# A two-layer trunk with expert gathers: scale rows spread by TensorE, six expert slots, two weight buffers, seven kept chunks

## The chip, the core and the metric

The kernel runs on one core of a Trainium2 chip. The metric is the device time of one execution in microseconds (us). A change of 0.2% (3.6 us) is about what a measurement of this kernel can tell from none.

## What is computed

The reference is one inference step of two layers for 256 prompt tokens and 32 sample tokens (model width 1024, all float32). Each layer is a token mixer followed by an expert mixer. Cut to what matters:

```python
# layer 0: chunk_mlp_mixer                      # layer 1: short_conv_mixer
z = gelu(rms_norm(x, norm_mix) @ w_in)          b_gate, c_gate, h = split(rms_norm(x, norm_mix) @ w_in, 3)
u, v = split(z, 2)                              z = c_gate * h
v = layer_norm(v, ln_g, ln_b)                   zp = concatenate([buf, z])
mixed = einsum('gij,bcjgd->bcigd', ws, v) + bias  conv = sum(conv_w[k] * zp[:, k:k + s_len] for k in range(3))
x = x + (u * mixed) @ w_out                     x = x + (b_gate * conv) @ w_out

def peer_ffn(h, ...):        # h = rms_norm(x, norm_ffn); both layers; every token, 8 heads, 16 experts of each
    q = h @ w_query                     # 8 heads x 2 halves x 128
    s = q . sub_keys                    # 128 scores per half
    idx, g = top 16 of the sums of the two halves' top 16, softmax
    a = gelu(sum over d of expert_u[idx] * h)
    x = x + sum over heads and k of g * a * expert_v[idx]
y = rms_norm(x, norm_final)
```

Outputs are y, the normalised v rows of the sample tokens, and the last two rows of the convolution's input for both groups.

## The kernel before

**Tiles and passes.** Tokens stand on partitions in three tiles: 0 and 1 with 128 prompt tokens each, 2 with the 32 sample tokens. The dense work is done in four passes: layer 0 for tile 0, layer 0 for tiles 1 and 2, then layer 1 in the same way (`PASSES`). Each pass streams its layer's weight matrices as chunks of 1024 x 256 floats, 1 MiB each: 32 chunks in layer 0 (8 for v, 8 for u, 8 for the way out, 8 for the queries), 24 in layer 1 (12 for b, c and h, 4, 8).

**Where weights lie.** `kept` holds the first chunk of a layer for both passes of the layer (`KEEP = 1`). All others go through `wring`, three buffers of 1 MiB; SyncE issues each load as soon as TensorE has used the chunk three places earlier (`load_chunk`, line 527). Before the experts start, chunks 1 to 5 of the first pass lie in slots of `uvring`.

**Experts.** Each of 576 items (tile, head, rank) is a gather by GpSimd of 128 rows of 8 KB (an expert's u and v side by side), 1 MiB in all, into one of seven slots of `uvring` (`RING = 7`, line 585). For an item VectorE takes the dot product of u and the token (`dot`, line 1139), ScalarE its gelu (line 879), VectorE makes a small diagonal matrix of the weight (line 1152), and TensorE adds weight times v into PSUM (`weigh`, line 632; line 624 for tile 2). Then the slot is free, and GpSimd gathers the item seven places on.

**Order of the work.** The program runs in turns of two items (`TURNS`). `plan_steps` deals the dense work and the routing (top 16, softmax, indices) out over the turns before it is built: in each turn every engine first does its part of the two items and then dense steps up to a budget (`ROOM`). Each engine runs its list in order. In a turn TensorE's list is: two items' matmuls, then dense matmuls, typically one weight chunk. PSUM has six banks for the dense groups, used in rotation, and two for the experts' sum.

**Scale rows.** The gains of the root-mean-square norms come as broadcast DMAs of 512 KB (one row to 128 partitions) into `gain`, five in all (lines 554, 563, 564, 570, 894). Gain and bias of the layer norm of v come the same way: 1 MiB each for tile 0 into two slots of `uvring`, and for tiles 1 and 2 in halves into `ln_half`, whose second half ScalarE's queue loads only once VectorE has used the first (`ln_load`, the step `ln load`); VectorE waits for it in `lnapply` (lines 1060 and 1063). A norm is a sum of squares (`nstat`), a root on ScalarE, and `napply` (line 1035). The bias of the mixing matrix is a matmul of `ones` with `brow`.

**Names of the dense steps.** `v`, `vq`, `vf` are the products for v (`vq` the sample tokens' in quarters of the array, `vf` the sum of the quarters); `u`, `bch`, `q` go through `blocks` (line 643), two blocks to a chunk; `mix` is the mixing over positions, `out`, `oq`, `of` the way out (line 747), `xT` a transpose, `s` the scores.

Of the kernel before, what the change touches and what calls it, by code (L numbers as in the profile page):

```python
# [39 lines left out]
WRING = 3  # L40
# [11 lines left out]


KEEP = 1
EARLY = KEEP + 5
RINGED = [n for n in range(EARLY, PASS_CHUNK0[-1]) if n - max(p for p in PASS_CHUNK0 if p <= n) >= KEEP]

RING = 7  # L60
# [5 lines left out]
PAIRS = len(ITEMS) // 2  # L66
END = {(l, t): (ITEM0[l, t] + TILE_ITEMS[t]) // 2 - 1 for l, t in ITEM0}
# [29 lines left out]
def mixer_steps(n):  # L97
# [22 lines left out]
    if l == 0:  # L120
# [11 lines left out]
        for b in range(KA):  # L132
            out.append(("PE", ("u", n, b), blk, [x_read]))
            out.append(("ACT", ("u read", n, b), 0.35, [("u", n, b)]))
            if b == 0:
# [6 lines left out]
                for h in range(2):  # L142
                    for t in tiles:
                        out.append(("DVE", ("lnapply", t, h), 2.8, [("root", "ln", 0, t), ("ln load", n, h)]))
                    if n == 1 and h == 0:
                        out.append(("ACT", ("ln load", n, 1), 0.1, [("lnapply", tiles[-1], 0)]))
# [32 lines left out]
    if 2 in tiles:  # L179
        out.append(("ACT", ("spread", l), 3.2, [("napply", "ffn", l, 2)]))  # L180
# [22 lines left out]
def final_steps(t):  # L203
    return [("DVE", ("nstat", "final", 1, t), 1.5, [("vdone", 1, t)]),
            ("ACT", ("root", "final", 1, t), 1.6, [("nstat", "final", 1, t)]),
            ("DVE", ("napply", "final", 1, t), 1.6, [("root", "final", 1, t)])]
# [5 lines left out]
        "mix": "gate", "out": "add", "vq": "vq read", "vf": "vf read", "oq": "oq read", "of": "add"}  # L212
# [23 lines left out]
def plan_steps():  # L236
# [3 lines left out]
    norms = [s for s in early if not s[1][0].startswith("xT")]  # L240
# [13 lines left out]
    turn = {("start",): -2, ("ln load", 0, 0): -2, ("ln load", 0, 1): -2, ("ln load", 1, 0): -2}  # L254
# [1018 lines left out]
```

## Time and profile before

| what | value |
|---|---|
| median of 3 runs | 1820.49 us (1819.88 to 1820.83) |
| the profiled execution | 1821.85 us, span 1820.0 us |
| moved by DMA | 733.21 MB, mean 403 GB/s |
| TensorE busy | 1334.9 us (73%) |
| VectorE busy | 1218.0 us (67%) |
| ScalarE, GpSimd busy | 290.2 us, 683.7 us |
| mean granted TensorE clock | 0.79 of full speed |

Busy times of different engines overlap. The profile's page gives each engine's busy share in 40 slices of the span, the bytes that each DMA queue moved, and the chain of work that ended last. A busy TensorE is not one at its peak. "Idle before" an instruction is the time that its engine stood still, with what ended it.

### The profile page before, as it was taken

To read this page: it belongs to the slowest core of one execution; us is meant where nothing else is said; L and a number is where in the kernel's file an instruction comes from. 1 tells how busy PE (TensorE), PEld (TensorE's weight loads), DVE (VectorE), ACT (ScalarE), POOL (GpSimd) and SP (SyncE) were. 2 spreads that over 40 slices of the span, in tenths; PEclk is the share of its full clock that TensorE was granted. 3 is DMA by queue.
4 is the path that set the end of the run, shared out by engine and by line. 5 is a ranking of instruction groups with operands and counts; after the bars stand their busy time and mean duration, and the time that the engine had idled before them with its cause. 6 is when DMAs were issued, how large, how long until landed. Compare 5 with 4: busy or idle time off the path is not lost.

```text
span 1820.0 us, 22838 instructions
## 1 busy us (share of the span) xinstructions
PE 1334.9 (73%) x8328; PEld 636.3 (35%) x8328; DVE 1218.0 (67%) x3189; ACT 290.2 (16%) x972; POOL 683.7 (38%) x580
## 2 busy tenths in 40 slices
PE   7996988978847888766664598878766667776743
PEld 6984546535502554421111175346211111111100
DVE  1338676756679577688887646656888975555565
ACT  1112221103202102111121111031111110000011
POOL 0013332343334333334445533443544444444453
PEclk9998999998967988976665599989766666666655
DMA  9779999999999999999999999999999999999996
GB/s 352 276 276 422 421 421 393 398 421 421 420 421 385 419 421 421 421 419 401 421 421 390 399 416 421 422 420 421 402 421 409 412 422 421 421 421 417 418 412 278
DMA packets 103267, 733.21 MB, mean 403 GB/s; under 512 B 12305, under 2 KB 12817, under 8 KB 14930
## 3 DMA queue, kind: packets, MB, share of 16 engines
q0 software_dynamic: 82944, 604.02, 80.4%
q1 hardware_dynamic: 19442, 125.82, 17.2%
q10 hardware_dynamic: 768, 1.91, 0.3%
q8 instruction: 66, 1.08, 0.2%
q14 instruction: 47, 0.39, 0.1%
HBM read 730.19 MB, written 1.52 MB: 402 GB/s over the span
## 4 chain that ended last, share of the span: by engine, by line
DMA 56%; PE 26%; DVE 8%; issue 7%; DVEq 2%; POOL 2%; ACT 0%; ACTq 0%; POOLq 0%
DMA uvring<-expert_uv_dram,idx 54%; PE psum L632 11%; PE psum L643 7%; PE psum L747 3%; PE psum L675 2%; POOL uvring L585 2%; DVE diag L1152 1%; DVE uvring L1139 1%; DMA arena<-ln_bias_dram 1%; DVEq L953 1%; PE psum L624 1%; PE psum L727 1%; DVE ti L955 1%; PE psum L730 1%; PE psum L665 0%
## 5 line engine op out<-in xcount | busy, mean ns | idle before, releaser
L585 POOL DMA_INDIRECT uvring<-expert_uv_dram,idx x576 | 683.5, 1187 | 1114.5 <-PE psum L632 878.2
L1139 DVE SCALAR_TENSOR_TENSOR uvring<-uvring,xn 128x1024 f32<-128x1024 f32 x576 | 705.7, 1225 | 458.9 <-DMA uvring<-expert_uv_dram,idx 448.5
L632 PE MATMUL psum<-uvring,diag 64*64 64x512 f32 x4096 | 725.7, 805 | 367.8 <-DVE diag L1152 358.4
L632 PEld LDWEIGHTS psum<-uvring,diag 64*64 64x64 f32 x4096 | 134.6, 159 | 872.5 <-DVE diag L1152 811.3
L879 ACT ACTIVATE a_gelu<-a_raw 128x1 f32<-128x1 f32 x576 | 116.6, 203 | 1335.4 <-DVE uvring L1139 1334.9
L643 PEld LDWEIGHTS psum<-xT,wring 128*128 128x128 f32 x2240 | 296.1, 200 | 50.8 <-issue 47.4
L643 PE MATMUL psum<-xT,wring 128*128 128x128 f32 (+1 forms) x2240 | 309.9, 299 | 3.2 <-ACT arena L798 2.0
L1152 DVE TENSOR_SCALAR diag<-twin,a_gelu,gate 128x64 f32<-128x64 f32 x512 | 159.1, 311 | 0.4 <-ACT a_gelu L879 0.4
L624 PE MATMUL psum<-uvring,diag 128*32 128x256 f32 x512 | 67.8, 624 | 91.7 <-DVE diag L1152 85.6
L747 PE MATMUL psum<-wring,arena 128*128 128x256 f32 x384 | 88.4, 387 | 0.6 <-issue 0.6
L747 PEld LDWEIGHTS psum<-wring,arena 128*128 128x128 f32 x384 | 72.2, 192 | 21.9 <-issue 12.5
L798 ACT ACTIVATE arena<-psum 128x128 f32<-128x128 f32 (+2 forms) x164 | 45.9, 301 | 119.7 <-PE psum L643 78.9
L624 PEld LDWEIGHTS psum<-uvring,diag 128*32 128x32 f32 x512 | 13.0, 139 | 145.9 <-DVE diag L1152 137.9
L1139 DVE DVE_READ_ACCUMULATOR uvring<-uvring,xn 128x1 f32 x576 | 47.4, 82 | 0.0
L879 ACT ACT_TABLE_LOAD x29 | 37.2, 1283 | 0.5
L675 PE MATMUL psum<-wring,xT 128*128 128x256 f32 x144 | 33.1, 385 | 0.0
L675 PEld LDWEIGHTS psum<-wring,xT 128*128 128x128 f32 x144 | 26.9, 190 | 7.8 <-issue 4.5
L1044 DVE BATCH_NORM_STATS2 stats<-arena 128x6 f32<-128x512 f32 (+1 forms) x12 | 7.4, 674 | 32.2 <-ACT arena L798 32.2
L1118 DVE TENSOR_TENSOR x<-x,psum 128x256 f32<-128x256 f32 (+1 forms) x24 | 9.9, 412 | 27.6 <-PE psum L747 27.6
L665 PE MATMUL psum<-ident,xn 128*128 128x128 f32 (+1 forms) x96 | 16.7, 329 | 12.0 <-DVE xn L1035 11.9
L873 ACT ACT_TABLE_LOAD x19 | 24.4, 1283 | 0.3
L1072 DVE TENSOR_TENSOR arena<-arena,psum 128x256 f32<-128x256 f32 (+1 forms) x16 | 7.0, 452 | 25.7 <-PE psum L730 25.7
(104 smaller groups left out, 718.8 us busy)
## 6 DMA issues: line engine op xcount, KB each, us to landing
wring<-w_chunks_dram SPq DMA_DIRECT2D x103, 1024.0 KB, 9.5
uvring<-expert_uv_dram,idx POOLq DMA_INDIRECT x576, 12.0
uvring<-w_chunks_dram SPq DMA_DIRECT2D x5, 1024.0 KB, 13.9
kept<-w_chunks_dram SPq DMA_DIRECT2D x2, 1024.0 KB, 10.8
gain<-gains_dram SPq DMA_DIRECT2D x4, 512.0 KB, 13.1
x<-x_tok_dram SPq DMA_DIRECT2D x2, 512.0 KB, 5.0
uvring<-ln_gain_dram SPq DMA_DIRECT2D x1, 1024.0 KB, 26.6
uvring<-ln_bias_dram SPq DMA_DIRECT2D x1, 1024.0 KB, 27.4
```

What stands on the lines that cost most here:

```text
L585: pool.indirect_dma_start(uvring[:, n % RING, :], None, expert_uv, bass.IndirectOffsetOnAxis(ap=idx[t][:, i:i + 1], axis=0),).then_inc(uv_ ...
L624: mm = nc.tensor.matmul(acc[32 * q:32 * q + 32, 0:256], diag[:, place % DIAGS, 0:32], row[:, D + 256 * q:D + 256 * (q + 1)], start=first, ...
L632: mm = nc.tensor.matmul(acc[64 * j:64 * j + 64, 512 * i:512 * (i + 1)], diag[64 * i:64 * i + 64, place % DIAGS, :], row[64 * i:64 * i + 64 ...
L643: mm = nc.tensor.matmul(bank(key, WIDTH[n]), w[:, k, j * P:(j + 1) * P], act[:, k, 0:cols], start=(k == 0), stop=(k == KD - 1))
L675: mm = nc.tensor.matmul(bank(k, WCOLS, ROWS[t]), xT[:, kk, LCOL[t]:LCOL[t] + ROWS[t]], w[:, kk, :], start=(kk == 0), stop=(kk == KD - 1))
L727: nc.tensor.matmul(both[:, :, cols], ones[0:r, :], bias, start=True, stop=False)
L747: mm = nc.tensor.matmul(bank(key, WCOLS, ROWS[t]), act[:, h * KD + kk, LCOL[t]:LCOL[t] + ROWS[t]], w[:, kk, :], start=(h == 0 and kk == 0) ...
L798: nc.scalar.activation(out, bank(key, n, rows), func).then_inc(scalar_read, 1)
L873: nc.scalar.activation(gate[t][:, c], gate[t][:, c], ACT.Exp, accum_out=esum[t][:, h:h + 1]).then_inc(exp_done, 1)
L879: nc.scalar.activation(a_gelu[:, c:c + 1], a_raw[:, c:c + 1], ACT.Gelu_apprx_tanh).then_inc(gelu_done, 1)
L1139: nc.vector.scalar_tensor_tensor(out=uvring[:, slot, 0:D], in0=uvring[:, slot, 0:D], scalar=1.0, in1=xn[t][:, :], op0=ALU.mult, op1=ALU.mu ...
L1152: nc.vector.tensor_scalar(diag[:, place % DIAGS, 0:32 if t == 2 else 64], fold[:, :] if t == 2 else twin[:, :], a_gelu[:, c:c + 1], gate[t ...
```

## The change

1. **Scale rows by TensorE.** One DMA of 256 KB on ScalarE's queue puts all the rows (five gains, the layer norm's gain and bias in halves, the mixing bias) into 64 unused partitions of `x[2]`, the `table`. A matmul with one column of the identity, broadcast, as the stationary side spreads 512 elements of a row over 128 partitions of a PSUM bank (steps `gb` for gains, `lnb` for the layer norm of tiles 1 and 2). `napply` and the new `lnrow` read the scale from PSUM; `lnrow` does tiles 1 and 2 together, 512 columns at a time. The gain broadcasts and the halves of the layer norm's rows are gone. Tile 0 keeps its layer norm broadcasts.
2. **Smaller arena.** `gain`, `ones`, `brow`, `tril`, `zeros`, `quarters` and `ln_half` are gone or lie in other buffers; v of tile 2 lies in kept chunk 0; the convolution's product is made in place and two columns are carried from tile 0 to tile 1.
3. **Weights.** `KEEP` goes from 1 to 7, `WRING` from 3 to 2, `RING` from 7 to 6. `plan_homes` puts chunks 7 to 23 of the first pass, and chunk 26, in the slots of `uvring` and in the two buffers in turn; GpSimd waits for the last chunk of a slot before its first gather there.
4. `quarters` shares `turned`, so ScalarE waits for the readers of the one before it writes the other.

```diff
-WRING = 3
+WRING = 2
-KEEP = 1
-EARLY = KEEP + 5
+KEEP = 7
-RING = 7
+RING = 6
+def plan_homes():
+    places = [("slot", s) for s in range(2, RING)] + [("ring", r) for r in range(WRING)]
+    home, uses, ringed = [], {}, 0
+    for n in range(PASS_CHUNK0[-1]):
+        c = n - max(p for p in PASS_CHUNK0 if p <= n)
+        if c < KEEP:
+            at = ("kept", c)
+        elif n < 24:
+            at = places[(n - KEEP) % len(places)]
+        elif n == 26:
+            at = ("slot", RING - 1)
+        else:
+            at, ringed = ("ring", ringed % WRING), ringed + 1
...
     def norm(which, behind):
...
-            out.append(("DVE", ("napply", which, l, t), 1.6, [("root", which, l, t)]))
+        for j in range(2):
+            out.append(("PE", ("gb", which, l, tiles[0], j), 0.9, []))
+            out.append(("DVE", ("napply", which, l, tiles[0], j), 0.7 * len(tiles),
+                        [("gb", which, l, tiles[0], j), ("root", which, l, tiles[-1])]))
...
+            if n == 1 and 3 <= b < 11:
+                q, a = divmod(b - 3, 2)
+                out.append(("PE", ("lnb", q, a), 0.9, []))
+                out.append(("DVE", ("lnrow", q, a), 1.4, [("lnb", q, a), ("root", "ln", 0, 2)]))
...
+            def row_of(r, cols):
+                pe.wait_ge(ident_landed, 16)
+                pe.wait_ge(rows_landed, 16)
+                return ident[64:P, 64 + r:65 + r].to_broadcast([64, P]), table[:, cols]
...
+                    open_group(k)
+                    matrix, values = row_of(r, slice(j * 512, (j + 1) * 512))
+                    nc.tensor.matmul(bank(k), matrix, values, start=True, stop=True).then_inc(group_done, 1)
...
+                    wait_group(dve, key)
+                    if a == 1:
+                        after(steps[0])
+                        dve.wait_ge(vector_read, G["lnb", q, 0][3])
+                    for t in (1, 2):
+                        r = ROWS[t]
+                        done = nc.vector.scalar_tensor_tensor(
+                            out=v[t][0:r, cols], in0=v[t][0:r, cols],
+                            scalar=rstd[0:r, t:t + 1] if a else mv[0:r, t, 0:1], in1=bank(key, rows=r),
+                            op0=ALU.mult if a else ALU.subtract, op1=ALU.add if a else ALU.mult)
...
-            act.dma_start(gain[:, 0, :], gains[0:1, :].partition_broadcast(P)).then_inc(gain_landed[0], 16)
+            act.dma_start(table, rows).then_inc(rows_landed, 16)
```

**SyncE's queue.** These are its loads from the first 42 in a row to the last gain row, before: the rest of the first two passes' chunks, two gain rows, layer 1's keys and chunks.

```order
L527 DMA wring<-w_chunks_dram 128x2048 x42
L563 DMA gain<-gains_dram 128x1024
L564 DMA gain<-gains_dram 128x1024
L566 DMA keys<-sub_keys_dram 128x2048
L522 DMA kept<-w_chunks_dram 128x2048
L527 DMA wring<-w_chunks_dram 128x2048 x46
L570 DMA gain<-gains_dram 128x1024
```

The same place now:

```order
L557 DMA uvring<-w_chunks_dram 128x2048
L557 DMA wring<-w_chunks_dram 128x2048 x30
L582 DMA keys<-sub_keys_dram 128x2048
L557 DMA kept<-w_chunks_dram 128x2048 x7
L557 DMA wring<-w_chunks_dram 128x2048 x34
L587 DMA y_tok_dram<-xn 128x1024 x2
```

Seven kept chunks are loaded together behind the keys, then 34 through the ring where there were 46. Over the whole program 98 chunks are loaded instead of 110.

**TensorE's list in pass two, the start of the products for v**, before (line 632 is two items' matmuls in one turn):

```order
L675 MATMUL psum<-kept,xT 128x256 x8
L651 MATMUL psum<-kept,xT 32x256 x8
L632 MATMUL psum<-uvring,diag 64x512 x8
L675 MATMUL psum<-wring,xT 128x256 x8
L651 MATMUL psum<-wring,xT 32x256 x8
L632 MATMUL psum<-uvring,diag 64x512 x8
```

and now (line 649 is the former 632):

```order
L692 MATMUL psum<-kept,xT 128x256 x8
L668 MATMUL psum<-kept,xT 32x256 x8
L649 MATMUL psum<-uvring,diag 64x512 x8
L692 MATMUL psum<-kept,xT 128x256 x8
L668 MATMUL psum<-kept,xT 32x256 x8
L649 MATMUL psum<-uvring,diag 64x512 x8
```

The order is the same, and the chunk comes from `kept` for the first seven.

**TensorE's list in pass two, the products for u, now**, where the `lnb` matmuls (line 731) stand:

```order
L660 MATMUL psum<-xT,wring 128x160 x8
L731 MATMUL psum<-x,ident 128x512
L660 MATMUL psum<-xT,wring 128x160 x8
L649 MATMUL psum<-uvring,diag 64x512 x8
L731 MATMUL psum<-x,ident 128x512
L660 MATMUL psum<-xT,wring 128x160 x8
L731 MATMUL psum<-x,ident 128x512
```

Eight such matmuls come between the blocks, where before there was none; a turn has one or two of them.

## Rows read from the trace of the kernel before

**Rows 1.** The page: DMA share in 40 slices, bytes
```profile
DMA  9779999999999999999999999999999999999996
...
DMA packets 103267, 733.21 MB, mean 403 GB/s; under 512 B 12305, under 2 KB 12817, under 8 KB 14930
```

**Rows 2.** The page: the chain that ended last, by engine
```profile
DMA 56%; PE 26%; DVE 8%; issue 7%; DVEq 2%; POOL 2%; ACT 0%; ACTq 0%; POOLq 0%
```

**Rows 3.** Stretches: length, busy by engine, TensorE's clock, DMA share, GB/s
```profile
0.00:128.50 128.50, 113.24 (x703) 103.56 (x704) 38.12 (x110) 20.13 (x48) 0.21 (x5) 0.99 0.80 296
128.50:1808.00 1679.50, 1218.89 (x7607) 532.19 (x7609) 1173.85 (x3067) 267.30 (x918) 683.45 (x576) 0.78 1.00 414
...
1500.00:1600.00 100.00, 71.80 (x320) 10.98 (x312) 58.18 (x118) 7.91 (x39) 42.40 (x39) 0.61 1.01 421
```

**Rows 4.** Stretches of dense work in passes two, two, three and four
```profile
172.90:250.60 77.70, 73.93 (x532) 42.32 (x528) 54.22 (x155) 16.73 (x53) 27.25 (x24) 1.00 1.01 420
250.60:335.10 84.50, 71.39 (x484) 49.80 (x480) 57.37 (x134) 15.22 (x48) 24.22 (x23) 0.91 0.99 406
567.30:663.80 96.50, 83.25 (x616) 57.09 (x616) 65.55 (x183) 17.32 (x62) 30.48 (x28) 0.87 0.99 405
1031.40:1128.60 97.20, 88.05 (x616) 60.72 (x616) 52.68 (x135) 15.83 (x60) 35.23 (x28) 0.92 0.99 409
```

**Rows 5.** Stretches between them, where layer 1's chunks are loaded ahead
```profile
492.00:552.00 60.00, 31.98 (x152) 5.62 (x152) 42.17 (x120) 7.79 (x27) 20.51 (x18) 0.60 1.01 418
776.00:800.00 24.00, 15.99 (x105) 7.14 (x104) 17.05 (x53) 2.50 (x11) 7.88 (x7) 0.78 1.01 421
```

**Rows 6.** TensorE's timeline: two blocks in pass four, two items in pass three
```profile
1052.51 4.62 PE L643 MATMUL psum<-xT,wring 128*128 128x160 f32 x32
590.86 1.95 PE L632 MATMUL psum<-uvring,diag 64*64 64x512 f32 x16
```

**Rows 7.** VectorE's timeline at the layer norm's second half
```profile
289.33 1.28 DVE L1060 SCALAR_TENSOR_TENSOR arena<-arena,mv 128x1024 f32<-128x1024 f32 x1 [11.46 <-DMA arena<-ln_bias_dram]
```

**Rows 8.** DMA issues between 1031.4 and 1128.6 us, median time to landing
```profile
wring<-w_chunks_dram SPq DMA_DIRECT2D x11, 1024.0 KB, 9.1
```

**Rows 9.** Time to landing, chunk at 106.9 us, then chunk at 189.2 us
```profile
DMA to landing us min/median/max: 4.7/4.7/4.7
...
DMA to landing us min/median/max: 9.2/9.2/9.2
```

**Rows 10.** Gathers at 1500 to 1600 us, then the gather at 335.1 us
```profile
DMA to landing us min/median/max: 10.8/11.1/12.0
DMA to landing us min/median/max: 6.5/6.5/6.5
```

**Rows 11.** Timeline at 1528 us: a dot product, and the gather it leads to
```profile
1528.39 1.23 DVE L1139 SCALAR_TENSOR_TENSOR uvring<-uvring,xn 128x1024 f32<-128x1024 f32 x1 [1.02 <-DMA uvring<-expert_uv_dram,idx]
...
1532.19 0.95 POOL L585 DMA_INDIRECT uvring<-expert_uv_dram,idx  x1 [1.77 <-PE psum L632]
```

**Rows 12.** TensorE's timeline: the first transposes, and those before the queries
```profile
9.32 1.97 PE L665 MATMUL psum<-ident,xn 128*128 128x128 f32 x8 [9.32 <-DVE xn L1035]
109.48 1.31 PE L665 MATMUL psum<-ident,xn 128*128 128x128 f32 x8 [2.58 <-DVE xn L1035]
```

**Rows 13.** TensorE's timeline: one product of 512 columns (two records)
```profile
194.57 1.05 PE L702 MATMUL psum<-quarters,fold 128*32 128x512 f32 x2
```

**Rows 14.** Stretches with the DMA engines below their rate, columns as in rows 3
```profile
330.00:350.00 20.00, 18.40 (x125) 9.69 (x123) 15.54 (x50) 1.60 (x7) 5.35 (x6) 0.91 0.96 367
570.00:580.00 10.00, 6.94 (x40) 2.25 (x36) 9.78 (x32) 2.39 (x7) 3.23 (x3) 0.56 0.82 316
960.00:970.00 10.00, 6.36 (x48) 2.39 (x48) 9.62 (x20) 3.80 (x10) 5.83 (x6) 0.67 0.85 301
1040.00:1050.00 10.00, 10.00 (x61) 5.87 (x54) 7.02 (x15) 1.44 (x7) 6.98 (x4) 0.68 0.81 306
1270.00:1280.00 10.00, 10.00 (x71) 6.99 (x70) 8.11 (x14) 2.26 (x9) 3.32 (x3) 0.92 0.89 356
```

More of the change, by code:

```diff
@@ L141, in mixer_steps @@
                     out.append(("ACT", ("root", "ln", 0, t), 1.6, [("lnstat", t)]))
[L142 to L146, printed above, removed]
+                for h in range(2 if n == 0 else 0):
+                    out.append(("DVE", ("lnapply", 0, h), 2.8, [("root", "ln", 0, 0)]))
+            if n == 1 and 3 <= b < 11:
+                q, a = divmod(b - 3, 2)
+                out.append(("PE", ("lnb", q, a), 0.9, []))
+                out.append(("DVE", ("lnrow", q, a), 1.4, [("lnb", q, a), ("root", "ln", 0, 2)]))
         if n == 0:
@@ L211 @@
 READ = {"xT": "xT read", "v": "v read", "u": "u read", "bch": "bch read", "q": "q read", "s": "s read",
-        "mix": "gate", "out": "add", "vq": "vq read", "vf": "vf read", "oq": "oq read", "of": "add"}
+        "mix": "gate", "out": "add", "vq": "vq read", "vf": "vf read", "oq": "oq read", "of": "add",
+        "gb": "napply", "lnb": "lnrow"}
 def group_of(k):
@@ L244, in plan_steps @@
     ahead = first[:cut] + route_steps(0, 0, 0)
-    at = [k for _, k, _, _ in ahead].index(("out", 0, 0, 0, 0))
-    ahead[at:at] = norms
-    dense = first[cut:] + [s for s in early if s not in norms]
+    at = [k for _, k, _, _ in ahead].index(("xT read", 0, "ffn", 0, 1)) + 1
+    ahead[at:at] = stats
+    dense = first[cut:] + [s for s in early if s not in stats]
     dense += [s for s in mixer_steps(1) if s not in early] + mixer_steps(2) + mixer_steps(3)
@@ L316 @@
 EXPS = [h for k in planned("ACT", ("exp",)) for h in ((k[1], k[2], k[3] + j) for j in range(dict(calls_of(*k[1:3]))[k[3]]))]
-FORM = {r: g for g, r in READ.items() if r not in ("gate", "add")}
+FORM = {r: g for g, r in READ.items() if r not in ("gate", "add", "napply", "lnrow")}
 PE_STEPS = tuple(READ)
@@ L326, in plan_groups @@
     vector = {}
-    for k in planned("DVE", ("gate", "add")):
-        vector[("of", *k[1:3]) if k[0] == "add" and k[3] == 2 else
-               ("mix" if k[0] == "gate" else "out", *k[1:])] = len(vector) + 1
+    form = {"gate": "mix", "add": "out", "napply": "gb", "lnrow": "lnb"}
+    for k in planned("DVE", tuple(form)):
+        vector[("of", *k[1:3]) if k[0] == "add" and k[3] == 2 else (form[k[0]], *k[1:])] = len(vector) + 1
     for k in planned("PE", PE_STEPS):
```

271 lines of the change are left out of this document (136 added, 135 removed).

## The prediction

> **What bounds the kernel now.** I read the page first, then stretches by engine, then timelines where two engines meet. The page shows the DMA engines nearly full in almost every slice after the fourth [rows 1], and the chain that ended last is 56% DMA, 26% TensorE [rows 2]. Split at the first gather, 128.5 us, the stretches say more [rows 3]. Before it DMA moves 296 GB/s and TensorE is busy 113 of 128.5 us: the first pass waits for TensorE. From there to 1808 us DMA moves 414 GB/s, and 421 where nothing else happens, so 421 is the rate here and 1 MiB takes 2.49 us. Only 1679.5 x (1 - 414/421) = 28 us of DMA time are unused there.
>
> That reads as a DMA-bound kernel, but the dense stretches have a second bound right behind it [rows 4]. TensorE is busy 73.9 of 77.7 us where v is computed in pass two, 71.4 of 84.5 in the u part, 83.3 of 96.5 and 88.1 of 97.2 where b, c and h are computed in passes three and four. A turn there is 4.62 us of blocks and 1.95 us for two items [rows 6], about 6.5 us, while its two gathers and one chunk need 3 x 2.49 = 7.5 us of DMA. With the chunk kept, DMA needs 5.0 us and TensorE still 6.5. So bytes taken from a dense turn give back at most 1 us of their 2.49, and bytes moved out of it into a stretch with gathers alone cost all 2.49.
>
> **The change part by part.** It takes out twelve chunks (12.58 MB) and nine broadcasts of 0.524 MB, and adds 0.26 MB: 17.0 MB, 40.5 us of DMA. What that is worth, place by place, in us, with both ends:
>
> *Start and first pass: +1.2 (0 to +3).* Two spreading matmuls stand ahead of the first transposes. A product of 512 columns takes 1.05 us [rows 13], and the first transposes run 1.97/1.31 = 1.5 times slower than later ones [rows 12], so 1.6 us each, partly beside the wait for x and VectorE's sum. The gain broadcast no longer competes with x. Later the first query chunk can only be loaded when the last chunk of the way out is used, at 106.9 us; it lands 4.7 us later [rows 9], 111.6, about when the queries start (transposes at 109.48 plus some 2 us). The gain matmuls there run while TensorE waits for the norm. DMA bytes before 128.5 us are not on the path.
>
> *One chunk less ahead of the v part: -1.5 (-2.5 to 0).* Two buffers are filled there, not three; VectorE is also busy.
>
> *v part: -3 (-3.8 to 0).* The kept chunks leave TensorE's list as it was, and it has 3.8 us of idle time [rows 4].
>
> *u part and layer norm: -4 (-4.7 to 0).* VectorE's wait of 11.46 us for the bias half [rows 7] goes with its DMA. Eight spreading matmuls add 8 x 1.05 = 8.4 us to TensorE: 79.8 of 84.5. `lnrow` costs VectorE about 1 us more in shorter instructions, hidden (57.4 busy of 84.5). What is late next is TensorE.
>
> *Three gain rows after the first gather: -3.7.* 3 x 0.524 MB at 421 GB/s, in full stretches. The other two gain rows and the first two layer norm halves lie before 128.5 us: nothing.
>
> *Layer 1's chunks loaded ahead: +12.4 (+10 to +12.4).* Behind the keys SyncE now issues seven kept and two ring chunks, where it issued one and three. DMA moves 418 GB/s there [rows 5], so five more cost 5 x 2.49. They come out of the next stretch.
>
> *b, c, h in pass three: -9.5 (-13.2 to -5).* Of about eleven loads there five remain, beside the 28 gathers (POOL, [rows 4]): 28 + 5 transfers are 82 us, TensorE's 83.3 is the floor under 96.5. I take 87, since both engines are near full and take turns at waiting.
>
> *One ring chunk less before pass four: -2.5*, at 421 GB/s [rows 5].
>
> *b, c, h in pass four: -4.5 (-9.1 to 0).* Eleven loads [rows 8] become five, TensorE's floor is 88.1 of 97.2; more of it is one engine's work in a row than in pass three.
>
> *Six slots: +8 (0 to +12.4).* In the gather-only stretch a landed item leads to the next gather 3.8 us later (1528.39 to 1532.19, [rows 11]), which lands 11.1 us after its issue [rows 10]: 14.9 us for six items, because an item's slot is freed only after the next item's dot product. With six slots it is 12.4 us for five items, so the landing may take 8.6 us. A gather behind an empty queue took 6.5 [rows 10], so the steady state holds, with 2.1 us to spare where it had 4.6. Where VectorE is late by more, the DMA engines stand still: they lost 12 us in five places before [rows 14], by their GB/s against 421. Each can grow by one slot, 5 x 2.49 = 12.4. I take two thirds, as one of the five is the layer norm's wake.
>
> *Two weight buffers: +2 (0 to +8).* A chunk beside gathers lands after 9.2 us even when it is the only one asked for, against 4.7 without gathers [rows 9]. Two turns must cover its landing and its own use: (9.2 + 4.6)/2 = 6.9 us, a little over TensorE's 6.5 and under DMA's 7.5. About ten turns run at TensorE's pace: 10 x 0.4 = 4, half of it absorbed. The Trainium skill (DMA: Bandwidth & Descriptors, Queues, rings and completion order) says that each DMA engine serves the queues that have work in rotation, packet by packet. By that rule a lone chunk beside gathers would take about twice its transfer time, two buffers would cost nothing and the sum would be 2 us lower; no row here shows such a short landing beside gathers, so the row's value stands.
>
> Sum: 1.2 - 1.5 - 3 - 4 - 3.7 + 12.4 - 9.5 - 2.5 - 4.5 + 8 + 2 = **-5.1 us**. The profiled execution took 1821.85 us (span 1820.0) and would take 1816.8; against the median of the runs, 1820.49, it is **1815.4 us**.
>
> **The rivals.**
>
> *All bytes count.* DMA is the only bound, and TensorE's busy time shrinks with fewer stalls. For it: 421 GB/s everywhere, and TensorE's records stretch where its clock is low (0.87 in pass three, [rows 4]). Against it: 73.9 of 77.7 us at a clock of 1.00. After the first gather eleven chunks and five broadcasts go, 14.2 MB, 33.6 us; with 1.2 at the start it gives 1788 us.
>
> *Slower: the sixth slot was needed.* The place is the loop of [rows 11], in every item. It decides from the landing of a gather with five slots in flight: above 8.6 us each item costs a fifth of the excess. Lowest seen is 6.5 after an empty queue, but a chunk beside gathers needs 9.2. At 8.8 us it is 0.04 x 576 = 23 us; with the other terms less the 8 already in, -13.1 + 23 gives 1830 us. Late routing on VectorE works the same way. For it: VectorE's 9.6 to 9.8 of 10 us busy where DMA runs dry [rows 14]. Against it: the spare 2.1 us.
>
> *The rows from TensorE are waited for.* `lnrow` and `napply` stand in VectorE's list and now wait for a matmul that stands behind a turn of dense work on TensorE; dot products queue behind them. If that eats the u part's gain, the same time is lost at six norms, 1 us each: 4 + 6 = +10 less what is hidden, about 1820 us, no change. It is also the case in which the change does not do what it says: the broadcasts' wait is only replaced.
>
> **How the numbers follow.** The forecast gets 0.46 (own range 1806 to 1822; 0.36 of it faster, 0.10 within), all bytes 0.16, the sixth slot 0.28, the replaced wait 0.10 (0.04 within, 0.06 slower). Of the sixth slot's cases 0.01 end within. The bound for faster and slower is 0.2%, 3.6 us, about what a measurement of this kernel can tell from no change: faster 0.52, same 0.15, slower 0.33. The range 1796 to 1835 takes in the ends of the unknown terms; it leaves out most of the bytes case (0.12) and the top of the slower one (0.08).
>
> **What would show it.** Right: DMA moves about 716 MB; the v part keeps its length within 4 us with DMA well under 421 GB/s and TensorE full; 1031 to 1129 shortens by under 6 us; the wait for the bias half is gone; the stretch after the keys is 10 us and more longer; gathers land after some 8.6 us in the gather-only stretch, at 2.49 us an item. Wrong: the dense stretches shorten by 10 us and more each (bytes), or the gather-only stretch shows more than 2.5 us an item and GpSimd's gathers find idle DMA engines (sixth slot), or VectorE shows waits for line 731 of several us.

## The result, and the profile after

The changed kernel takes 1842.43 us (median of 4 runs, 1839.28 to 1848.51); the kernel before, on the same chip, 1820.18 us (4 runs, 1819.8 to 1820.83). The ratio is 1.012, with a 95% interval of 1.0103 to 1.0137: slower by 22 us, where 5 us less were forecast and the range ended at 1835.

The page after, whose first lines answer to [rows 1] and whose last one to [rows 2] (DMA share and GB/s in 40 slices, bytes, queues, chain by engine):

```profile
DMA  9749999899999999999999999999999999999997
GB/s 377 280 175 418 357 357 385 353 409 415 394 421 406 372 418 420 420 409 396 402 396 403 416 335 398 413 413 406 399 417 400 378 419 421 421 421 416 417 415 303
DMA packets 100369, 716.17 MB, mean 390 GB/s; under 512 B 12032, under 2 KB 12544, under 8 KB 13568
q0 software_dynamic: 82944, 604.02, 81.1%
q1 hardware_dynamic: 16896, 110.09, 14.8%
DMA 44%; PE 36%; DVE 9%; issue 8%; DVEq 2%; POOL 1%; ACT 0%; SPq 0%; POOLq 0%
```

The bytes came out as forecast, 716 MB. The rate did not hold: 390 GB/s in the mean where it was 403. At 421 GB/s the 17.0 MB saved would be 40 us, but the time in which the DMA engines stand idle grew by more than that. The span less the bytes at 421 GB/s is 1820.0 - 1741.6 = 78 us before and 1837.5 - 1701.1 = 136 us now.

Stretches, columns as in [rows 3]: up to the first gather, from there to the last, and 100 us of gathers alone.

```profile
0.00:130.00 130.00, 120.19 (x712) 103.84 (x713) 34.05 (x102) 20.12 (x48) 0.25 (x5) 1.00 0.71 276
130.00:1826.00 1696.00, 1235.94 (x7663) 541.17 (x7661) 1179.90 (x3083) 266.70 (x916) 681.06 (x576) 0.78 0.99 401
1520.00:1620.00 100.00, 69.32 (x324) 11.00 (x320) 59.00 (x121) 8.11 (x40) 44.09 (x40) 0.65 1.01 421
```

With gathers alone nothing is lost: 40 gathers in 100 us and 421 GB/s, as before. The loss is in the rest, 401 GB/s from 130 to 1826 us against 414.

For the place of it, take turns (two items each) and read when VectorE starts the dot product of a turn's first item. Lengths of the stretches between such turns in the profiled executions, in us; K is the number of kept chunks, W of weight buffers, R of slots. The rows below the second are the experiments.

| kernel (K, W, R) | to 0 | 0-16 | 16-32 | 32-56 | 56-64 | 64-80 | 80-144 | 144-160 | 160-216 | 216-287 | span |
|---|---|---|---|---|---|---|---|---|---|---|---|
| before (1, 3, 7) | 134.3 | 111.6 | 116.6 | 160.5 | 40.6 | 111.8 | 353.2 | 109.7 | 309.4 | 358.6 | 1820.0 |
| after (7, 2, 6) | 135.8 | 101.4 | 123.2 | 169.0 | 53.4 | 100.8 | 358.9 | 105.1 | 318.2 | 357.8 | 1837.5 |
| e1 (6, 3, 6) | 136.8 | 101.7 | 116.7 | 165.4 | 53.3 | 103.8 | 358.8 | 107.4 | 318.3 | 359.2 | 1835.0 |
| e2 (6, 2, 7) | 136.3 | 98.6 | 132.3 | 160.8 | 53.3 | 101.1 | 351.7 | 101.3 | 313.9 | 356.8 | 1820.1 |
| e3 (5, 3, 7) | 136.4 | 97.9 | 116.4 | 159.4 | 52.7 | 102.5 | 352.8 | 105.9 | 309.6 | 357.4 | 1805.0 |
| e4 (1, 3, 7) | 136.3 | 106.6 | 114.4 | 157.7 | 42.9 | 110.6 | 354.4 | 111.3 | 306.7 | 356.8 | 1811.7 |
| e5 (6, 2, 6) | 135.6 | 101.9 | 126.4 | 168.0 | 50.7 | 105.2 | 359.6 | 105.8 | 324.7 | 358.3 | 1850.2 |
| e7 (4, 3, 8) | 135.7 | 100.6 | 125.0 | 154.7 | 50.9 | 103.0 | 354.1 | 104.1 | 309.2 | 357.5 | 1808.9 |
| e8 (5, 3, 7) spread | 135.8 | 97.6 | 127.5 | 159.1 | 41.6 | 104.6 | 352.4 | 105.9 | 311.2 | 357.2 | 1807.0 |
| e10 (5, 2, 7) | 135.8 | 98.1 | 127.8 | 161.6 | 50.2 | 101.3 | 353.8 | 102.9 | 314.4 | 356.5 | 1816.5 |
| e11 (4, 4, 7) | 134.5 | 103.5 | 123.3 | 156.4 | 53.3 | 105.3 | 352.2 | 106.2 | 306.3 | 357.1 | 1812.0 |
| e12 (1, 2, 6) | 136.9 | 112.7 | 121.9 | 164.5 | 40.7 | 112.8 | 361.9 | 111.0 | 317.8 | 358.3 | 1852.2 |
| e6 before, six slots | 133.2 | 117.7 | 116.9 | 164.4 | 41.9 | 116.6 | 353.6 | 111.4 | 317.5 | 358.4 | 1845.4 |
| e9 before, two buffers | 153.3 | 112.1 | 121.7 | 159.7 | 40.0 | 113.2 | 351.8 | 110.5 | 312.4 | 357.6 | 1845.9 |

Turns 0 to 32 hold pass two's dense work, 64 to 80 pass three's, 144 to 160 pass four's; layer 1's chunks are loaded in 56 to 64; 216 to 287 are gathers alone. After against before: 0 to 16, 64 to 80 and 144 to 160 get shorter (-10.2, -11.0, -4.6), 56 to 64 grows by 12.8, and 16 to 32, 32 to 56, 80 to 144 and 160 to 216 grow by 6.6, 8.5, 5.7 and 8.8. The forecast had a gain for the first, and for all the places of [rows 14] together no more than the 8 us of the slots.

Two waits. VectorE from 240 to 300 us, where [rows 7] had 11.46 us for the bias half, and TensorE's chunk matmuls in all, then in 135 to 375 us:

```profile
DVE uvring L1190 <- DMA uvring<-expert_uv_dram,idx: 15.4, 10, 3.4
DVE arena L1109 <- PE psum L731: 2.5, 3, 1.2
DVE diag L1203 <- ACT a_gelu L908: 0.3, 1, 0.3
```
```profile
PE psum L660 <- DMA wring<-w_chunks_dram: 21.0, 14, 4.1
...
PE psum L660 <- DMA wring<-w_chunks_dram: 10.7, 4, 4.1
```

The wait for the bias is gone, and what takes its place is 2.5 us for the spreading matmul. But TensorE now waits 21.0 us for chunks, half of it in the u part. So there were three suspects: two buffers, six slots, or the rows from TensorE with their new order.

### The profile page after: what moved, and what is told of

Read it like the earlier page. It is cut to its first block, busy times and chain, and to the rows that moved or that the text cites. A ratio compares the mean times of both kernels' runs of the same rounds, so it can differ in the third digit from the quotient of the medians.

```text
span 1837.5 us, 22998 instructions
## 1 busy us (share of the span) xinstructions
PE 1358.2 (74%) x8388; PEld 645.6 (35%) x8388; DVE 1220.0 (66%) x3197; ACT 289.6 (16%) x970; POOL 681.3 (37%) x580
## 4 chain that ended last, share of the span: by engine, by line
DMA 44%; PE 36%; DVE 9%; issue 8%; DVEq 2%; POOL 1%; ACT 0%; SPq 0%; POOLq 0%
DMA uvring<-expert_uv_dram,idx 39%; PE psum L660 12%; PE psum L649 12%; DMA wring<-w_chunks_dram 4%; PE psum L779 4%; PE psum L692 3%; DVE uvring L1190 2%; DVE diag L1203 2%; PE psum L731 1%; PE psum L641 1%; PE psum L762 1%; PE psum L759 1%; PE psum L668 1%; POOL uvring L601 1%; DVE ti L998 1%
## 5 line engine op out<-in xcount | busy, mean ns | idle before, releaser
L649 PE MATMUL psum<-uvring,diag 64*64 64x512 f32 x4096 | 709.0, 795 | 337.5 <-DVE diag L1203 325.5
L908 ACT ACTIVATE a_gelu<-a_raw 128x1 f32<-128x1 f32 x576 | 116.6, 203 | 1320.2 <-DVE uvring L1190 1307.6
L660 PE MATMUL psum<-xT,wring 128*128 128x160 f32 (+1 forms) x1632 | 228.8, 299 | 22.4 <-DMA wring<-w_chunks_dram 21.0
L660 PEld LDWEIGHTS psum<-xT,wring 128*128 128x128 f32 x1632 | 215.4, 197 | 63.6 <-issue 29.9
L779 PE MATMUL psum<-wring,arena 128*128 128x256 f32 x304 | 76.0, 407 | 1.8 <-issue 1.0
L828 ACT ACTIVATE arena<-psum 128x160 f32<-128x160 f32 (+2 forms) x160 | 45.8, 295 | 148.0 <-PE psum L660 107.5
L660 PEld LDWEIGHTS psum<-xT,kept 128*128 128x128 f32 x448 | 56.1, 191 | 11.8 <-issue 9.7
L660 PE MATMUL psum<-xT,kept 128*128 128x128 f32 (+1 forms) x448 | 59.2, 291 | 0.4 <-ACT xT L846 0.4
L692 PE MATMUL psum<-kept,xT 128*128 128x256 f32 x224 | 52.5, 394 | 0.8 <-ACT xT L846 0.8
L692 PEld LDWEIGHTS psum<-kept,xT 128*128 128x128 f32 x224 | 43.4, 197 | 11.9 <-issue 6.0
L731 PE MATMUL psum<-x,ident 64*128 64x512 f32 x60 | 34.1, 684 | 6.0 <-DMA ident<-ident_c_dram 6.0
```

What stands on the lines that cost most here:

```text
L649: mm = nc.tensor.matmul(acc[64 * j:64 * j + 64, 512 * i:512 * (i + 1)], diag[64 * i:64 * i + 64, place % DIAGS, :], row[64 * i:64 * i + 64 ...
L660: mm = nc.tensor.matmul(bank(key, WIDTH[n]), w[:, k, j * P:(j + 1) * P], act[:, k, 0:cols], start=(k == 0), stop=(k == KD - 1))
L692: mm = nc.tensor.matmul(bank(k, WCOLS, ROWS[t]), xT[:, kk, LCOL[t]:LCOL[t] + ROWS[t]], w[:, kk, :], start=(kk == 0), stop=(kk == KD - 1))
L731: nc.tensor.matmul(bank(k), matrix, values, start=True, stop=True).then_inc(group_done, 1)
L779: mm = nc.tensor.matmul(bank(key, WCOLS, ROWS[t]), act[:, h * KD + kk, LCOL[t]:LCOL[t] + ROWS[t]], w[:, kk, :], start=(h == 0 and kk == 0) ...
L828: nc.scalar.activation(out, bank(key, n, rows), func).then_inc(scalar_read, 1)
```

## The experiments

Times are medians; a difference "to before" is taken with the kernel before in the same series on the same chip (1821.58, 1822.47, 1823.4 and 1820.89 us for e1-e4, e5-e8, e9-e11, e12). The changed kernel has room for 15 units of 8 KB a partition as kept chunks, buffers and slots, so e1 to e3 trade one against another. The intervals are wide beside the smaller effects: some 7 us either way for e1, 2 to 6 for the others, so a difference of two runs under some 5 us is not clear of the noise.

### e1: the third buffer back

```diff
-WRING = 2
+WRING = 3
-KEEP = 7
+KEEP = 6
```

> The changed kernel with three weight buffers again, paid for with one kept chunk less (six kept, six slots for expert rows). Theory 1, the two weight buffers cost most of the loss: the changed kernel's TensorE waits 21 us in sum for chunks of the weight ring, and its turns 16 to 56 lost 15 us where 8 us of gain were forecast; most of it comes back, and the time falls by 12 to 22 us to 1820 to 1830 us, with the wait for chunks at lines 660 and 731 under 8 us. Theory 2, the six slots cost most of it: the time falls by less than 6 us (over 1836 us). Theory 3, the rows spread by TensorE and the new order of the steps cost it: also less than 6 us. The kept chunk that is given up is worth under 2 us by all of them.

1838.09 us (1834.61 to 1849.5), ratio 1.0107 (1.0067 to 1.0147), 16.5 to before. Only 5.7 of the 22 us come back, less than theory 1 had said. The waits are gone (the matmul's idle time of 22.4 us becomes 2.5), so the buffers may matter, but they are not the main cause:

```profile
L660 PE MATMUL psum<-xT,wring 128*128 128x160 f32 (+1 forms) x1728 | 239.2, 297 | 2.5 <-ACT arena L828 1.4
```

### e2: the seventh slot back

```diff
-KEEP = 7
+KEEP = 6
-RING = 6
+RING = 7
```

> The changed kernel with seven slots for expert rows again, paid for with one kept chunk less (six kept, two weight buffers). Theory 2, the six slots cost most: turns 80 to 144 and 160 to 216, where gathers run with little beside them, lost 15 us; they come back, and the time falls by 12 to 18 us to 1824 to 1830 us. Theory 1, the two weight buffers: the time falls by less than 6 us, and the waits of TensorE for chunks of the weight ring stay at about 20 us. Theory 3: less than 6 us.

1817.66 us (1813.2 to 1824.76), ratio 0.9984 (0.9963 to 1.0006). One slot for one kept chunk is worth 26 us, more than theory 2 had said.

### e3: both back

```diff
-WRING = 2
+WRING = 3
-KEEP = 7
+KEEP = 5
-RING = 6
+RING = 7
```

> The changed kernel with three weight buffers and seven slots, paid for with two kept chunks (five kept). By theories 1 and 2 together the losses of both come back: 1842 less 15 to 20 for the buffers and 8 to 15 for the slots is 1807 to 1819 us, faster than the kernel before. By theory 3, the rows spread by TensorE or the order of the steps as the cause, it stays over 1830 us.

1806.17 us (1803.08 to 1811.68), ratio 0.9918 (0.9893 to 0.9944): faster than the kernel before by 15 us, a little under the expected range, and with e7 the best of the study. Theory 3 alone would have left it over 1830. Its page, in the same lines:

```profile
GB/s 382 296 162 422 383 412 420 404 416 421 409 423 401 393 421 421 420 421 415 420 409 400 420 351 421 412 421 419 406 419 410 390 420 422 422 421 420 422 416 281
DMA packets 100945, 720.37 MB, mean 399 GB/s; under 512 B 12096, under 2 KB 12608, under 8 KB 13632
```

It moves 4.2 MB more than the changed kernel, 10 us of DMA, and is 38 us faster (15.4 under the kernel before, where the changed one is 22.3 over it).

### e4: the change without the trade

```diff
-WRING = 2
+WRING = 3
-KEEP = 7
+KEEP = 1
-RING = 6
+RING = 7
```

> The changed kernel with the memory as it was: one kept chunk, three weight buffers, seven slots, so that only the rows spread by TensorE, the smaller arena and the new order of the steps are left of the change. Theories 1 and 2: the loss was in the memory that was traded, so this is at or a little under the kernel before, 1810 to 1822 us. Theory 3: over 1828 us. Against the run with five kept chunks it tells what four more kept chunks are worth: the prediction's terms say 12.4 x 4/6 of loss at the keys against (9.5 + 4.5) x 4/6 of gain in passes three and four, so within 2 us of each other.

1813.25 us (1812.81 to 1815.89), ratio 0.9957 (0.9941 to 0.9974). Theory 3 falls: the rows from TensorE, the smaller arena and the new order together save 8.3 us. Which of them does it was not tested. Its second part missed: four more kept chunks (e3 against e4) are worth 7.1 us, not within 2.

### e5: six kept, two buffers, six slots

```diff
-KEEP = 7
+KEEP = 6
```

> The changed kernel with one kept chunk less and nothing for it: six kept, two weight buffers, six slots, so that it differs from the run with the seventh slot by the slot alone and from the run with the third buffer by the buffer alone. Theory 2, refined: the seventh slot is worth 22 to 28 us and the third buffer 2 to 6, the seventh kept chunk under 3, so 1840 to 1846 us. Rival: the seven kept chunks themselves were the loss in the changed kernel, and giving one up is what both runs gained by: then 1825 to 1836 us.

1848.96 us (1844.21 to 1853.45), ratio 1.0137 (1.0106 to 1.0167), 26.5 to before. That is over the 1840 to 1846 us expected. Against e2 this is one slot alone: 30.4 us (22 to 28 expected). Against e1 it is one buffer alone: 10.0 us (2 to 6 expected), a difference that is hardly clear of e1's wide interval. The seventh kept chunk comes out at 4.2, which is not clear of the noise. The rival, seven kept chunks as the loss, is out.

The slot's mechanism can be read here. About the same piece of the program, turns 104 to 112 (routing, items, no chunk loads), first with six slots, then with seven (columns as in [rows 3]); the second line of each is 5 us inside it:

```profile
838.00:880.00 42.00, 26.24 (x126) 4.88 (x128) 35.49 (x109) 3.99 (x17) 18.80 (x16) 0.62 0.96 387
864.00:869.00 5.00, 4.24 (x24) 0.75 (x16) 4.85 (x13) 0.41 (x2) 3.12 (x3) 0.65 0.59 206
```
```profile
832.00:872.00 40.00, 23.34 (x128) 4.51 (x128) 35.68 (x109) 3.82 (x17) 20.04 (x15) 0.71 1.01 418
856.00:861.00 5.00, 4.18 (x28) 0.86 (x24) 4.81 (x14) 0.59 (x3) 3.24 (x3) 0.84 1.03 411
```

DMA falls to 206 GB/s in the one and stays at 411 in the other. The timelines of VectorE, TensorE and GpSimd with six slots say why (start, length, in brackets the idle time before and its releaser):

```profile
856.59 0.09 DVE L992 MATCH_VALUE_LOAD scores<-tv,scores 128x8 f32 x1
...
859.60 0.29 DVE L998 FIND_INDEX8 ti<-tv,scores 128x8 uint32<-128x128 f32 x1
859.96 1.23 DVE L1190 SCALAR_TENSOR_TENSOR uvring<-uvring,xn 128x1024 f32<-128x1024 f32 x1
```
```profile
856.73 1.98 PE L649 MATMUL psum<-uvring,diag 64*64 64x512 f32 x8 [0.26 <-DVE diag L1203]
861.48 6.77 PE L649 MATMUL psum<-uvring,diag 64*64 64x512 f32 x32 [2.77 <-DVE diag L1203]
869.68 1.09 PE L649 MATMUL psum<-uvring,diag 64*64 64x512 f32 x8 [1.44 <-DVE diag L1203]
```
```profile
859.02 0.94 POOL L601 DMA_INDIRECT uvring<-expert_uv_dram,idx  x1 [1.31 <-PE psum L649]
865.26 1.77 POOL L601 DMA_INDIRECT uvring<-expert_uv_dram,idx  x1 [5.31 <-PE psum L649]
867.34 0.94 POOL L601 DMA_INDIRECT uvring<-expert_uv_dram,idx  x1 [0.30 <-PE psum L649]
```

From 856.59 to 859.89 VectorE finds top values for the next head, and the dot product behind it starts only at 859.96, 3.4 us after the first of them. TensorE then takes 1.98 us an item at a low clock, where it takes 1.09 at full clock. No slot comes free, and GpSimd issues nothing for 6.2 us (859.02 to 865.26). With six slots that empties the queue. With seven one more gather lies in it, and the longest pause of GpSimd's at this place is 4.3 us. A part of this one place is TensorE's clock and not the slot: over the 42 and 40 us it is 0.62 in the one and 0.71 in the other. Counted in slices of 1 us, over turns 32 to 144 and 160 to 216, spells in which at least 0.5 us of transfer at 421 GB/s is missing: e5 has 31 with 34.8 us, e2 has 11 with 9.8 us. These turns are 21 groups of 16 items, so with six slots most groups have a spell. The 25 us between the two kernels are most of the 30. How many spells there are depends on the shortfall from which a slice counts; that six slots have at least twice as many does not.

The kernel before and e6, which differ by the slot alone, show that the engines are late about as often, and that the ring decides what it costs. In the same turns GpSimd's issues lie more than 4 us apart 76 times before and 80 times in e6, and at most 7.2 and 7.3 us apart, at a mean granted clock of 0.79 and 0.78; spells, with slices from a tenth short, are 9 with 11 us before and 22 with 23 us in e6.

The steady state is as the prediction had it. Gathers from 1560 to 1660 us, issue to landing, with six slots and then, for e2, with seven; both at 421 GB/s:

```profile
uvring<-expert_uv_dram,idx POOLq DMA_INDIRECT x41, 8.6
```
```profile
uvring<-expert_uv_dram,idx POOLq DMA_INDIRECT x40, 11.4
```

### e6: the kernel before with six slots

```diff
-EARLY = KEEP + 5
+EARLY = KEEP + 4
-RING = 7
+RING = 6
```

> The kernel before with six slots instead of seven and nothing else (one chunk of the first pass goes to the weight ring instead of a slot). Theory: a slot less costs wherever TensorE or VectorE is late by more than the ring covers, in the kernel before as in the changed one: 22 to 32 us more, 1842 to 1852 us, with most of it in the dense stretches and little between turns 232 and 280. Rival: the sixth slot was only missed because two weight buffers made TensorE late: under 10 us more, 1821 to 1831 us.

1847.86 us (1842.83 to 1852.87), ratio 1.0138 (1.0107 to 1.0169), 25.4 to before. The slot's price is no matter of this change's other parts. In the profiled executions 12.6 us of it lie in turns 0 to 16, 64 to 80 and 144 to 160, where TensorE is dense, and 12.0 in 32 to 56 and 160 to 216; "most in the dense stretches" was half right. Turns 216 to 287 give none of it (358.4 against 358.6).

### e7: eight slots

```diff
-WRING = 2
+WRING = 3
-KEEP = 7
+KEEP = 4
-RING = 6
+RING = 8
```

> The changed kernel with four kept chunks, three weight buffers and eight slots. If a slot buys cover for the time that the engines are late, an eighth buys less than the seventh but still some: 5 to 12 us off the run with seven slots and five kept (1806.2), less 2 for the kept chunk, so 1796 to 1803 us. Rival: with seven the queue is full nearly everywhere (its slices show 400 to 421 GB/s), and an eighth is worth nothing: 1806 to 1810 us.

1806.41 us (1802.08 to 1810.69), ratio 0.9901 (0.9879 to 0.9924): the same as e3, with one kept chunk less. The rival's number, but not cleanly: the profiled execution lost 8.6 us against e3 in turns 16 to 32, where TensorE's clock fell (last section), and after turn 32 it is 6.8 us shorter than e3. Whether an eighth slot is worth a few us stays open.

### e8: layer 1's kept chunks loaded earlier

e3, with kept chunks 1 to 4 of layer 1 loaded between pass two's chunks:

```diff
             for n in range(PREFETCHED, PASS_CHUNK0[2]):
                 load_chunk(n)
+                if PASS_CHUNK0[1] + 10 <= n < PASS_CHUNK0[1] + 9 + KEEP:
+                    load_chunk(PASS_CHUNK0[2] + n - PASS_CHUNK0[1] - 9)
...
-            for n in range(PASS_CHUNK0[2], PASS_CHUNK0[4]):
+            for n in (PASS_CHUNK0[2], *range(PASS_CHUNK0[2] + KEEP, PASS_CHUNK0[4])):
```

> The changed kernel with five kept chunks, three buffers and seven slots, and the kept chunks of layer 1 but the first loaded one by one between the chunks of pass two's u and out parts instead of in a row behind the keys. The loads in a row delayed the gathers by 12 us between turns 56 and 64. Theory A: the queue has slack in pass two, where it moves 391 to 416 GB/s, and part of the 10 us of these four chunks comes for nothing: 1796 to 1803 us. Theory B: bytes cost the same wherever they go, since gathers are behind all the time: 1804 to 1808 us, with the loss moved to turns 24 to 48.

1807.7 us (1803.79 to 1814.04), ratio 0.9919 (0.9887 to 0.9951): theory B. Turns 56 to 64 shorten by 11.1 us (52.7 to 41.6) and turns 16 to 32 grow by 11.1 (116.4 to 127.5), somewhat earlier than the turns 24 to 48 expected. There was no slack; the gathers give way to the loads wherever those stand: from 266 to 296 us, at 421 and 419 GB/s, GpSimd issues 7 gathers where it issued 10 in e3.

### e9: the kernel before with two buffers

```diff
-WRING = 3
+WRING = 2
```

> The kernel before with two weight buffers instead of three and nothing else. Theory B: where TensorE runs one chunk after another (the u, q and b, c, h parts) it takes about 9.2 us a chunk (two blocks of 4.62) and a chunk lands 9 to 10 us after its issue beside gathers; with two buffers every late landing becomes a wait of TensorE, and its granted clock falls in it. Waits of the chunk matmuls for the weight ring go from near 0 to over 20 us, and the time rises by 8 to 20 us, to 1830 to 1842 us. Rival, the rule of the prediction (two buffers cost 2): 1820 to 1826 us.

1847.45 us (1842.5 to 1849.26), ratio 1.0124 (1.0102 to 1.0146), 24.1 to before: more than either theory allowed (8 to 20 us by theory B). 19.0 us of it lie ahead of turn 0, where this kernel's first pass loads all but six chunks through the ring; the changed kernel's slots avoid just that. The rest is mainly 5.1 us in turns 16 to 32 and 3.0 in 160 to 216. TensorE's wait is there, 48.9 us in sum:

```profile
PE psum L643 <- DMA wring<-w_chunks_dram: 48.9, 31, 5.8
```

### e10: two buffers with five kept chunks

```diff
-KEEP = 7
+KEEP = 5
-RING = 6
+RING = 7
```

> The changed kernel with five kept chunks and seven slots, as in the run with both back, but with two weight buffers: against that run (1806.2) the buffer alone. Theory B: 8 to 20 us more, 1814 to 1826 us, most of it lost in turns 16 to 32 (shorter by 15 or more us with three buffers in the pair compared so far) with the wait of line 660 for the weight ring at over 20 us. Rival: the third buffer gave nothing by itself, and the run with both back is fast for another reason: 1803 to 1810 us.

1817.13 us (1815.19 to 1824.15), ratio 0.9968 (0.9955 to 0.9981). Against e3 (to before: -6.3 and -15.4) the buffer costs 9.1 us; in the profiled executions turns 16 to 32 are 11.4 us longer, the spans differ by 11.5, and the other stretches cancel out. The stretch 234 to 300 us, with two buffers and with three:

```profile
234.00:300.00 66.00, 61.71 (x383) 38.76 (x385) 41.77 (x81) 16.90 (x44) 19.70 (x17) 0.95 0.95 386
```
```profile
234.00:300.00 66.00, 65.13 (x428) 40.90 (x428) 47.78 (x99) 17.35 (x47) 26.07 (x19) 1.00 1.01 420
```

One such wait in TensorE's timeline (e10):

```profile
309.02 2.44 PE L660 MATMUL psum<-xT,wring 128*128 128x160 f32 x16
314.05 3.98 PE L660 MATMUL psum<-xT,wring 128*128 128x160 f32 x16 [2.59 <-DMA wring<-w_chunks_dram]
```

TensorE waits 2.59 us, and the next sixteen matmuls take 3.98 us instead of 2.44, because its granted clock is 0.50 from 314.8 to 318.2 us. So it is with all three waits from the first product for v to the first of the mixing (1.92, 2.37 and 2.59 us): a stretch at 0.50 follows each, 10.2 us in sum, which costs half of that. This part of the program in e10 and then in e3:

```profile
189.30:322.90 133.60, 126.72 (x830) 78.95 (x826) 94.21 (x247) 27.33 (x82) 45.25 (x37) 0.96 0.96 383
190.00:312.10 122.10, 121.23 (x831) 74.67 (x827) 93.53 (x245) 26.72 (x80) 47.47 (x37) 1.00 0.99 403
```

It is 11.5 us longer: 6.0 us of idle time (6.9 against 0.9) and 5.1 us of clock. A late chunk is paid for twice, by its wait and by the slower work behind it. The waits for chunks in passes three and four (7.3 and 4.0 us) lengthen neither turns 64 to 80 nor 144 to 160. The wait of line 660 is 27.0 us in all, as expected.

### e11: four buffers

```diff
-WRING = 2
+WRING = 4
-KEEP = 7
+KEEP = 4
-RING = 6
+RING = 7
```

> The changed kernel with four kept chunks, four weight buffers and seven slots. With three buffers the chunk matmuls wait 2.0 us in sum for chunks, so a fourth buffer has nothing to take away; it lets one more chunk lie in the queue ahead of the gathers. Theory B: worth nothing, and one kept chunk less costs about 2: 1805 to 1811 us. Rival: as the third buffer gave 10 us or more, the fourth gives a few: 1798 to 1804 us, and this would be the best of the series.

1808.9 us (1805.55 to 1813.81), ratio 0.9913 (0.9889 to 0.9936): theory B, the fourth buffer is worth nothing that can be measured.

### e12: one kept chunk in the small memory

```diff
-KEEP = 7
+KEEP = 1
```

> The changed kernel with its two weight buffers and six slots but one kept chunk instead of seven: against the changed kernel (1842.4) it is the price of six kept chunks, against the run with one kept chunk and the memory as before (1813.3) that of the buffer and the slot together. If the parts add up, 1813 plus 11 for the buffer (run with two buffers of five kept chunks against that with three) plus 25 to 31 for the slot gives 1849 to 1855 us, and the six kept chunks are worth 7 to 13 us. Rival, the prediction's terms: the six kept chunks cost 12.4 and give back 14, so 1842 to 1846 us. A third case: with all chunks through two buffers the waits of TensorE multiply, over 1858 us.

1855.86 us (1851.69 to 1861.54), ratio 1.0196 (1.0169 to 1.0223), 35.0 to before, just over the 1849 to 1855 us expected and under the third case: the parts add up nearly. Slot and buffer together cost 43.3 us (e12 against e4), and singly 25.4 to 30.4 and 9.1 to 10.0. The six kept chunks are worth 12.7 us (the changed kernel against e12).

## Why the prediction was wrong

The change falls into three parts, each between measured kernels: the new code -8.3 us (e4), slot and buffer +43.3 (e12), six kept chunks -12.7; the sum is +22.3, since each part starts where the one ahead of it ends. The prediction's terms in the same groups are -6.5 (start +1.2, u part -4, gain rows -3.7), +6 (slots +8, buffers +2, one chunk less ahead of the v part -1.5, and before pass four -2.5), and -4.6 (v part -3, loads ahead +12.4, pass three -9.5, pass four -4.5). It had the parts and the signs; the middle one is short by 37 us, and the kept chunks' gain was 8 us too small.

*Six slots: +8 (0 to +12.4).* Failed, and its upper end too: 25.4 us (e6) to 30.4 (e5 against e2). The loop of [rows 11] was worked out well: 8.6 us was forecast as the landing the ring allows and is what the gathers take, at 421 GB/s. The step that failed is the next one: "Each can grow by one slot, 5 x 2.49 = 12.4". The five places of [rows 14] are where seven slots already ran dry most; they hold 12 of the 28 us that the prediction itself had counted as unused. A slot less also opens every place where seven were just enough, and most of those show no dry stretch in the trace of before: with seven slots 11 spells, with six 31 (e2 and e5), and 9 and 22 in the kernel before and e6. Looking for a dry queue could not find them; the view to read was how late VectorE and TensorE release a slot, as in the timelines of e5. The rival of the sixth slot named "late routing on VectorE" as working the same way, which is what happened in the place shown for e5 (its own sign, 9.6 to 9.8 of 10 us busy, holds for two of the five places of [rows 14]; in three it is TensorE that has next to no idle time), and its 1830 us came nearer than the forecast; but its own price and place, 0.04 us in every one of 576 items by the landing of gathers, were wrong: the landing did not go over 8.6 us, and the gather-only stretch lost nothing. That it came near is luck.

*Two weight buffers: +2 (0 to +8).* Too small: 9.1 us (e10) and 10.0 (e5 against e1). The rate, 6.9 us a turn against TensorE's 6.5, was near, but it was taken as a mean over ten turns and half absorbed. In the runs each late chunk in pass two is a wait of 2 to 4 us that the third buffer had covered, and TensorE works at half its clock for a while behind it, which the term had at nothing: in e10 5.1 us beside 6.0 of waiting. The Trainium skill (DMA: Bandwidth & Descriptors, Queues, rings and completion order) has the DMA engines turn from queue to queue at each packet, and the prediction drew from it that this term would be zero. The traces agree in so far as a chunk does not stand behind all the gathers: weight chunks land after 9.3 us with six slots (e1) and 9.6 with seven (e3), in the median, while gathers go from 9.3 to 11.8. They do not agree with a landing of twice the transfer time, some 5 us, and the term was not zero.

*One chunk less ahead of the v part, one ring chunk less before pass four: -1.5 and -2.5.* In e10 against e3 turns 56 to 64 are 2.5 shorter and 144 to 160 3.0, so they are there; turns 0 to 16 show none (+0.2), and 160 to 216 take 4.8 back.

*v part: -3 (-3.8 to 0).* The bound was TensorE's idle time in the v part [rows 4]. TensorE from its first product for v to its first block of u, in e4 with one kept chunk and in e3 with five:

```profile
189.70:252.10 62.40, 58.93 (x410) 32.65 (x406) 42.17 (x121) 12.51 (x39) 22.12 (x19) 0.97 1.01 421
190.00:246.90 56.90, 56.90 (x411) 32.13 (x407) 43.66 (x124) 12.81 (x40) 21.36 (x19) 1.00 0.97 383
```

The gain is 5.5 us. Most of it is the 3.5 us of idle time and, what the bound had left out, 3.4 us at a clock of 0.50 that followed a wait of 2.61 us and cost 1.7. Between the kernel before (59.6 us) and the changed one (56.9) it is 2.7, near the forecast; against e12 (69.4) it is 12.5. Turns 0 to 16, read at VectorE, shorten by more, 8.7 us for four chunks (e3 against e4) and 11.3 for six (after against e12), because VectorE also gets further ahead of TensorE, which reaches turn 16's items 5.3 us earlier in e3 (244.9 against 250.2 us); the u part on TensorE gains nothing (65.1 us in e4, 65.2 in e3).

*u part and layer norm -4, three gain rows -3.7, start +1.2.* Together -6.5 against e4's -8.3: near, with the parts not tested singly. On TensorE the u part, to the first matmul of the mixing, takes 65.1 us in e4 where it took 73.8 before, and its idle time falls from 13.2 to 0.7; the floor of 79.8 us was too high. The start is +2.0 (136.3 against 134.3), and turns 0 to 56 give 10.0. The spreading matmuls are waited for by VectorE for 2.5 us at the layer norm and 2.4 at the other norms: the rival of the replaced wait did not come true.

*Layer 1's chunks loaded ahead: +12.4.* Right: turns 56 to 64 cost 12.8 us, and 12.7 against e12.

*b, c, h in pass three -9.5 and in pass four -4.5.* Right: 11.0 and 4.6 against before, 12.0 and 5.9 against e12, inside their ends.

*All bytes count, 1788.* Not in the changed kernel. In e3, where ring and buffers stay deep, 12.8 MB less (30 us at 421 GB/s) give 15 us: half.

## What to carry to other kernels

Memory that keeps weights and memory that gives transfers room to run ahead have different prices: here a kept chunk is worth about 2 us, the third weight buffer 9 to 10 (24 in the kernel before, 19 of it in the first pass), the seventh slot 25 to 30, an eighth slot or a fourth buffer nothing that could be measured, which is to say less than some 5. What these runs suggest is to price a ring's depth by how late its consumers can be (the longest gap between two releases of a slot, on every engine that releases one), not by its steady state and not by where the queue runs dry today. Moving a load to another time is worth nothing while the queue has a gather waiting there (e8).

## What the runs showed of the hardware

TensorE's granted clock fell behind short waits (e10), and also while the profile shows it busy without a break, and a memory-bound kernel paid for it. In the mixing part of pass two, 340 to 350 us, e2 and then e3 (columns as in [rows 3]):

```profile
340.00:350.00 10.00, 10.00 (x40) 5.61 (x38) 5.75 (x17) 1.33 (x3) 2.23 (x2) 0.50 0.37 132
```
```profile
340.00:350.00 10.00, 10.00 (x82) 5.99 (x84) 4.77 (x11) 0.72 (x3) 1.88 (x2) 1.00 0.98 371
```

At 0.50, the 1.2 GHz level, TensorE does 40 matmuls in 10 us where it does 82 at 2.4 GHz, and DMA drops to 132 GB/s; that this is because the items' slots come free behind the dense work is the likely reason, not a tested one. In e7 TensorE was busy without idle time from 280 to 310 us at 1.00, and from 320 to 340 us, as busy, the clock was 0.50:

```profile
326.00:356.00 30.00, 30.00 (x134) 17.76 (x134) 15.35 (x34) 4.70 (x14) 7.28 (x7) 0.62 0.73 277
```

e3's profiled execution passed the same 30 us at 0.94 and 394 GB/s. In e7 the clock is 0.50 from 317.9 to 348.6 us, beginning 7 us into the mixing part, whose matmuls are small (128 x 128 and 32 x 32). Falls with no idle time ahead of them stand in the mixing part of the changed kernel, e1, e2, e4, e5, e7, e10 and e11, and not in that of the kernel before or of e3; why they differ stays open. Turns 16 to 32 of e7 are 8.6 us longer than e3's, and no wait for chunks is there to explain it. Such falls may be part of why runs of one kernel lie up to 15 us apart, those of the kernel before too (1817.76 to 1826.42 in one series); that was not tested. They also blur single stretches: turns 16 to 32 of e2, e7 and e11 hold the longest, so the slot is read from the stretches after turn 32 and from the medians.
